# A 28,000-instruction fp32 kernel on one core: the opening, the hand-over to the experts, and the places of the adaptive weights' quarters are rearranged

## What is computed

```python
h = concat([meta, x])                      # 16 + 256 tokens
u = rmsnorm(h, norm_mix_w)
proj = u @ w_in                            # 1024 -> 2064 columns
h = h + concat([pool_mixer(..), gla_mixer(..)]) @ w_out
h = h + hier_moe(rmsnorm(h, norm_ffn_w))   # 4 groups x 4 experts, top 1 group, top 2 experts
x = rmsnorm(h, final_norm_w)[:, 16:]
```

## Time and profile before

| | us |
|---|---|
| median of 3 runs | 2054.75 |
| the runs | 2054.5, 2054.75, 2058.7 |
| the profiled execution | 2057.1 |
| its span, first to last instruction | 2055.3 |
| PE busy in it | 1996.4 |
| DVE busy | 1409.0 |
| ACT busy | 816.3 |

### The profile page before, as it was taken

The page is one execution under the profiler, slowest core; times in us unless marked ns, Lnnn a source line. Parts: engine busy times, 40 slices in busy tenths (PEclk is TensorE's granted clock), DMA queues, the critical chain, the costliest instruction groups (busy, mean ns, idle before and its releaser), DMA issues.

```text
span 2055.3 us, 28217 instructions
## 1 busy us (share of the span) xinstructions
PE 1996.4 (97%) x11259; PEld 1702.3 (83%) x11259; DVE 1409.0 (69%) x1975; ACT 816.3 (40%) x1180; POOL 222.8 (11%) x129
## 2 busy tenths in 40 slices
PE   8989898999999999999999999999999999999998
PEld 7978677888888887579888888988888888689998
DVE  6879996778867569755778867566664346865444
ACT  5354575322222226954222222322222234764443
POOL 0010000000001002531000001000000101333431
PEclk9999999999999999999999999999999999999999
DMA  6557894556645353013656555356564336125654
GB/s 196 162 164 267 297 322 129 172 166 182 172 138 163 114 162 92 16 43 102 175 170 179 161 147 160 97 166 191 172 182 126 99 95 177 46 83 144 185 167 142
DMA packets 415032, 314.40 MB, mean 153 GB/s; under 512 B 27551, under 2 KB 373670, under 8 KB 414902
## 3 DMA queue, kind: packets, MB, share of 16 engines
q1 hardware_dynamic: 375344, 236.97, 39.5%
q10 hardware_dynamic: 39558, 75.64, 11.8%
HBM read 311.51 MB, written 1.05 MB: 152 GB/s over the span
## 4 chain that ended last, share of the span: by engine, by line
PE 85%; DVE 8%; ACT 4%; issue 2%; DMA 1%; ACTq 0%; SPq 0%; DVEq 0%
PE ps L2260 25%; PE ps L2262 24%; PE ps L2261 24%; DVE w_lo L1309 3%; PE ps L2253 2%; PE ps L3069 2%; ACT w_hi L770 2%; PE ps L3036 1%; DVE ada_acc L1335 1%; PE ps L2810 1%; PE ps L2812 1%; PE ps L2841 1%; PE ps L2811 1%; DVE u_lo L1402 1%; DVE tmp_a L1394 1%
## 5 line engine op out<-in xcount | busy, mean ns | idle before, releaser
L2260 PE MATMUL ps<-u_hi,w_hi 128*128 128x512 f32 (+2 forms) x2112 | 738.3, 350 | 13.1 <-DVE u_lo L1402 7.0
L2261 PE MATMUL ps<-u_lo,w_hi 128*128 128x512 f32 (+2 forms) x2112 | 728.5, 345 | 0.0
L2262 PE MATMUL ps<-u_hi,w_lo 128*128 128x512 f32 (+2 forms) x2112 | 728.5, 345 | 0.0
L1309 DVE TENSOR_TENSOR w_lo<-raw,w_hi 128x2048 fp32r<-128x2048 f32 (+1 forms) x215 | 451.5, 2101 | 222.2 <-ACT w_hi L770 222.1
L770 ACT CAST w_hi<-raw 128x2048 fp32r<-128x2048 f32 (+1 forms) x215 | 374.9, 1745 | 420.0 <-PE ps L2262 377.8
L2260 PEld LDWEIGHTS ps<-u_hi,w_hi 128*128 128x128 f32 x2112 | 401.0, 190 | 67.7 <-DVE w_lo L1309 8.5
L2262 PEld LDWEIGHTS ps<-u_hi,w_lo 128*128 128x128 f32 x2112 | 400.6, 190 | 47.9
L2261 PEld LDWEIGHTS ps<-u_lo,w_hi 128*128 128x128 f32 x2112 | 401.1, 190 | 46.0
L1335 DVE SCALAR_TENSOR_TENSOR ada_acc<-ada_w,sc_c,ada_acc 128x512 f32<-128x512 f32 x448 | 317.9, 764 | 6.3 <-DMA ada_w<-in_w_ada 0.7
L890 ACT ACTIVATE tmp_a<-ps 128x512 f32<-128x512 f32 (+1 forms) x88 | 47.9, 545 | 563.2 <-PE ps L2262 421.6
L2260 PE MATMUL ps<-hf_hi,w_hi 128*128 128x512 f32 (+1 forms) x770 | 268.7, 349 | 0.4 <-DVE w_lo L1309 0.2
(11 more groups left out here) (399 smaller groups left out, 2057.3 us busy)
## 6 DMA issues: line engine op xcount, KB each, us to landing
ada_w<-in_w_ada ACTq DMA_DIRECT2D x144, 512.0 KB, 3.8
raw<-in_w_ffn_gate SPq DMA_DIRECT2D x88, 512.0 KB, 3.9
raw<-in_w_ffn_up SPq DMA_DIRECT2D x88, 512.0 KB, 5.3
raw<-in_w_in SPq DMA_DIRECT2D x52, 512.0 KB, 4.8
raw<-in_w_ffn_down SPq DMA_DIRECT2D x64, 384.0 KB, 3.6
raw<-in_w_ffn_down SPq DMA_DIRECT2D x64, 320.0 KB, 4.2
raw<-in_w_expert_down SPq DMA_DIRECT2D x26, 512.0 KB, 5.9
raw<-in_w_expert_gate SPq DMA_DIRECT2D x25, 512.0 KB, 5.4
```

The lines of the kernel that those rows point to most:

```text
L1309: tt(low, full, high.bitcast(F32), ALU.subtract).then_inc(lo_done.sem, 1)
L2260: mm(acc, w1, m_hi, start=(first and i == 0), stop=False)
L2261: mm(acc, w1, m_lo, start=False, stop=False)
L2262: ins = mm(acc, w2, m_hi, start=False, stop=(last and i == n - 1))
```

## The change

It has five parts.

1. **Opening.** The weights of the first norm get a load of their own, first on ACT's queue, and their transpose goes with that of the meta rows. The products with ones are gone: ACT squares the rows as they were loaded and sums them in the same instruction, takes the root, DVE the reciprocal, and PE spreads it over the partitions with three small products. PE starts the first unit's high-by-high products as rows come, then transposes the vectors, then does the other two passes. The first unit's high part is made in two halves.
2. **Beside w_in.** Quarters 0 and 1 move from beside the seventh unit to behind the fifth; quarter 2 is done in halves around the head norm; both halves of quarter 3 come after it. A table load of ACT is moved ahead of a wait. The last chunk's output step is no longer cut in two.
3. **w_out.** The third unit is split in halves, and PE starts on the first.
4. **Experts.** Quarters: visit 0 has 5; visits 1, 2 and 3 had (6,7), (8,9) and (10,11,12) and get (6,7,8), (9,10,11) and (12,13,14); visits 4, 5 and 6 had one each and now visit 4 has 15. The loads follow.
5. **Last visits and hand-over.** Some context rows move behind the expert work. The first unit of the feed-forward network opens before the second tile is scattered, the second unit opens behind it by halves, too. The sums of squares move to DVE, and two small products are left of sixteen.

```diff
+            act.dma_start(mix_rows[:, :], dict(a["vec_src"])["norm_mix"]).then_inc(ld_mix, 16)
-            split_hi(0)
-            for k in range(KD):
-                act.wait_ge(rows_out.sem, rows_out.at(2 + k // 2))
-                nc.scalar.activation((win_a if k < 4 else win_b)[:, k % 4, PAD:PAD + T1], h1[:, k, 0:T1],
-                                     ACT.Square).then_inc(n0["sq"].sem, 1)
+            act.wait_ge(ev["mix_out"], 1)
+            open_rows(0, 2)
+            act.wait_ge(raw_full[0], 32)
+            nc.scalar.copy(w_hi[:, 0, 0:UNIT // 2], raw[:, 0, 0:UNIT // 2]).then_inc(ev["open_high"], 1)
+            open_rows(2, 4)
+            nc.scalar.copy(w_hi[:, 0, UNIT // 2:UNIT], raw[:, 0, UNIT // 2:UNIT]).then_inc(hi_done.sem, 1)
+            open_rows(4, KD)
+            for t, spare in enumerate((tmp_a, tmp_b)):
+                nc.scalar.activation(spare.rearrange("p a t -> p (a t)"), x_rows[:, t, :], ACT.Square, accum_out=tok_inv[:, 0, t:t + 1])
...
+            split_hi(1)
+            act.wait_ge(n0["spread"].sem, n0["spread"].at(1))
+            nc.scalar.copy(rstd[:, 0:T1], ps[:, 5, 0:T1]).then_inc(ev["open_factor"], 1)
...
+                if i == 4:
+                    dve.wait_ge(ev["sc_made"], 1)
+                    ada_quarter(0, 0)
+                    ada_quarter(0, 1)
@@ split_lo, and its like in split_hi
+                if u == OUT_THIRD:
+                    dve.wait_ge(ev["first_high"], 1)
+                    tt(low[:, 0:UNIT // 2], full[:, 0:UNIT // 2], high[:, 0:UNIT // 2].bitcast(F32), ALU.subtract).then_inc(ev["first_low"], 1)
+                    dve.wait_ge(hi_done.sem, u + 1)
+                    tt(low[:, UNIT // 2:UNIT], full[:, UNIT // 2:UNIT], high[:, UNIT // 2:UNIT].bitcast(F32), ALU.subtract
+                       ).then_inc(lo_done.sem, 1)
@@ the quarters' places
-        MOE_QUARTERS = (5, 6, 8, 10, 13, 14, 15, 16)
-        VISIT_LOADS = {1: (7, 8), 2: (9, 10), 3: (11, 12), 4: (13,), 5: (14,), 6: (15,)}
+        MOE_QUARTERS = (5, 6, 9, 12, 15, 16)
+        VISIT_LOADS = {1: (7, 8, 9), 2: (10, 11, 12), 3: (13, 14, 15)}
...
-                return [(q // 4, q % 4) for q in range(q0, q1)], {1: 0, 3: 1, 4: 2, 9: 3}.get(n)
+                return [(q // 4, q % 4) for q in range(q0, q1)], {1: 0, 2: 1, 3: 2, 9: 3}.get(n)
@@ ACT, last visits
-                    if v - 1 in CONTEXT_ROWS and v == VISITS - 1:
-                        high_rows("l0a", 0, 0, *CONTEXT_ROWS[v - 1])
-                if v == VISITS - 1:
-                    nc.scalar.activation(root_one[:, :], one, ACT.Sqrt)
...
-                if v - 1 in CONTEXT_ROWS and v < VISITS - 1:
+                if v - 1 in CONTEXT_ROWS:
                     high_rows("l0a", 0, 0, *CONTEXT_ROWS[v - 1])
             tile_high(TILES - 1)
+            nc.scalar.activation(root_one[:, :], one, ACT.Sqrt)
@@ DVE, hand-over
             for k in range(KD):
                 dve.wait_ge(ev["row_sums"], k + 1)
                 tt(h1[:, k, N_META:T1], row_sum(k), h1[:, k, N_META:T1], ALU.add).then_inc(acc_free.sem, 1)
-            split_lo(M1 + 1)
+                if k >= 2:
+                    square_sum(k - 1)
+            square_sum(KD - 1)
@@ PE, hand-over
+            scatter(2, 0, TILES - 1)
             turn_hidden((STEPS - 1,))
-            scatter(2, 0, TILES - 1)
             begin(down_unit(VISITS - 1), None)
             down_part(STEPS - 1, VISITS - 1, True)
             scatter(3, 0, TILES - 1)
+
+            u, g = layers[0]["f1a"]["u0"], layers[0]["f1a"]["g0"]
+            begin(u, None)
+            pe.wait_ge(ev["m_hid"], STEPS)
+            for k in range(KD):
+                open_ffn(0, 0, k)
             for k in range(4):
                 scatter(k, TILES - 1, TILES)
...
+            begin(u + 1, None)
+            pe.wait_ge(acc_free.sem, acc_free.at(st_moe["g0"] + 6))
+            for k in range(KD):
+                open_ffn(1, 0, k)
+                if k == 4:
+                    final_mean()
+            spread_factor("l0a", 0, 6, 1)
+            for i in range(2):
                 for k in range(KD):
-                    pe.wait_ge(n0["lo"].sem, n0["lo"].at(KD * q + k + 1))
...
+                    ins = open_ffn(i, 1, k)
+                ins.then_inc(unit_done.sem, 1)
```

More of the change, by code:

```diff
@@ L933, in _, with open_rows @@
-            act.wait_ge(n0["ms"].sem, n0["ms"].at(n0["n_ms"]))
-            nc.scalar.activation(rstd[:, 0:T1], ps[:, 5, 0:T1], ACT.Sqrt, bias=eps).then_inc(n0["root"].sem, 1)
-            split_hi(1)
+            def open_rows(k0, k1):
+                for k in range(k0, k1):
+                    act.wait_ge(rows_out.sem, rows_out.at(2 + k // 2))
+                    nc.scalar.activation(u_hi[:, k, 0:T1], h1[:, k, 0:T1], ACT.Identity, scale=mix_w[:, k:k + 1]
+                                         ).then_inc(n0["hi"].sem, 1)
@@ L1553, in _ @@
                                       ).then_inc(rows_out.sem, 1)
+            dve.wait_ge(rows_out.sem, rows_out.at(5))
+            dve.wait_ge(ev["mix_out"], 1)
+            mix1 = norm_of["mix1"]
+            for k in range(KD):
+                dve.wait_ge(mix1["hi"].sem, mix1["hi"].at(k + 1))
+                stt(out=u_lo[:, k, 0:T1], in0=h1[:, k, 0:T1], scalar=mix_w[:, k:k + 1], in1=u_hi[:, k, 0:T1].bitcast(F32),
+                    op0=ALU.mult, op1=ALU.subtract).then_inc(mix1["lo"].sem, 1)
@@ L1559, in _ @@
             ins.then_inc(rows_out.sem, 2)
-            split_lo(0)
-            dve.wait_ge(rows_out.sem, rows_out.at(8))
-            mix1 = norm_of["mix1"]
-            for k in range(KD):
-                w0 = VEC["norm_mix"][0] + k
-                dve.wait_ge(mix1["hi"].sem, mix1["hi"].at(k + 1))
-                stt(out=u_lo[:, k, 0:T1], in0=h1[:, k, 0:T1], scalar=vec[:, w0:w0 + 1], in1=u_hi[:, k, 0:T1].bitcast(F32),
-                    op0=ALU.mult, op1=ALU.subtract).then_inc(mix1["lo"].sem, 1)
@@ L1955, in _ @@
                         ada_quarter(*work[0])
+                    if v == VISITS - 1:
+                        for k in range(*CONTEXT_ROWS[v - 2]):
+                            low_row("l0a", 0, 0, k)
                     split_lo(u + 3)
-                    if v - 1 in CONTEXT_ROWS and v == VISITS - 1:
-                        for k in range(*CONTEXT_ROWS[v - 1]):
-                            low_row("l0a", 0, 0, k)
                 for i in steps_of(v):
@@ L1969, in _ @@
                 if v == VISITS - 1:
+                    for k in range(*CONTEXT_ROWS[v - 1]):
+                        scaled_row("l0a", 0, k)
                     hidden_low((STEPS - 1,))
@@ L2710, in turn_rows @@
                 return ins
-            for i in (2, 3):
+            pe.wait_ge(ev["first_low"], 1)
+            need(pe, acc_free, g + 1)
+            for t in range(2):
+                out1_part(2, t, 0, 4)
+            begin(u + 2, None)
+            for t in range(2):
+                ins = out1_part(2, t, 4, KD)
+            ins.then_inc(unit_done.sem, 1)
+            for i in (3,):
                 begin(u + i, g + i)
@@ L2858, in _, with final_mean, open_ffn @@
             n0, e1 = norm_of["l0a"], norm_of["end1"]
-            def final_mean(k):
-                pe.wait_ge(n0["sq"].sem, n0["sq"].at(k + 1))
+            def final_mean():
+                pe.wait_ge(ev["fin_sum"], KD - 1)
                 for t in range(2):
-                    ins = mm(ps[:, 4 + t, 0:1], square_row(k)[:, P * t:P * t + P], ones_d[:, 0:1], start=(k == 0),
-                             stop=(k == KD - 1))
-                ins.then_inc(ev["fin_means"], 1)
+                    ins = mm(ps[:, 4 + t, 0:1], sq_sum[:, SEQ + P * t:SEQ + P * t + P], ones_d[:, 0:1], start=True, stop=True)
+                ins.then_inc(ev["fin_mean"], 1)
+            def open_ffn(i, q, k):
+                u, (c0, c1, v) = layers[0]["f1a"]["u0"] + i, HALVES["l0a"][q]
+                if i == 0:
+                    pe.wait_ge(n0["lo"].sem, n0["lo"].at(KD * q + k + 1))
+                for t in range(2):
+                    ins = products(ps[:, 2 * i + t, c0:c1], u % 2, [up_cols(t, k)], [(u_hi[:, k, c0:c1], u_lo[:, k, c0:c1])],
+                                   c1 - c0, k == 0, k == KD - 1)
+                return ins
             pe.wait_ge(ev["places"], 1)
```

171 lines of the change are left out of this document (100 added, 71 removed).

## The result

The changed kernel takes 2043.66 us (median of 5 runs, 2043.14 to 2045.2) against 2054.75 for the kernel before beside it: a ratio of 0.9933, with a 95% interval of 0.9919 to 0.9948. The medians differ by 11.1 us. The profiled executions have spans of 2042.0 and 2055.3, 13.3 apart; 13.0 was forecast for them.

The account below looks back on a forecast made before the run. PE, busy 1996.4 of 2055.3 us, was taken as the bound, with gains only in its standing, half clock and needless products. Terms 2.2 + 2.1 + 2.0 + 2.8 + 3.9 = 13.0 gave 2042; range 2035.5 to 2049.

Parts of the forecast that it names:

- Opening: Start of the kernel: ACT's chain becomes the longest and unit 1 starts at 24.3 in place of 26.5, 2.2 us won.
- w_in to w_out: Hand-over between these weights: PE's waits of 1.40 and 1.56 for w_out's second and third units shrink, 2.1 us won.
- the 1.2 for the second unit: w_out's second unit: moving quarters 0 and 1 frees DVE earlier, winning 1.2 of PE's 1.40 wait.
- Together 4.3 us at the router, whose chain carries the shift on: Router: gains of the opening and w_out add to 4.3 us, and its latency-bound chain of small steps passes them on.
- Experts: Expert visits 2 to 7: new tables of quarters remove the 3.82 wait and half clock behind it, 2.0 us won.
- The five waits of 8.9: Expert visits 1 to 5: PE's waits of 0.7, 2.0, 2.8, 1.7 and 1.7, 8.9 against 7.4 before.
- half clock would be absent below 2.8: Expert visits: with none of the new waits over 2.8, visit 6's down product was taken to end 2.0 earlier.
- Last visit: Last expert visit: context rows go behind, and the down product starts at 325.9 in place of 329.09, 2.8 us won.
- Hand-over: Experts to feed-forward network: fill, clock and fewer small sums, less unit 1 in halves and three new waits, 3.9 us won.
- The three-quarter visits: Rival, chance 0.2: in visits 1 to 5 waits grow to 11 or 12, 3 lost in place of 2 won, 2047.
- The waits of the hand-over: Rival, chance 0.13: they only move, so last visit and hand-over give 2 or 3 of 6.7, 2046.
- DVE's debt: Slower rival, chance 0.04: in visits 5 to 15 DVE, over about 4 us behind PE, never catches up, 2059.

Follow-up runs that it names:

- sums_back: Changed kernel with the sixteen small sums of squares back on PE and DVE's seven additions of squares gone: 2047.11 us, ratio 0.9953.
- fill_back: Changed kernel with the first half unit of the feed-forward network behind the scatter in place of in front of it: 2047.58 us, ratio 0.9955.
- warm: Changed kernel with nineteen extra unread PE products in the router, before the norm's small sums and before the wait for the logits: 2041.37 us, ratio 0.9919.
- third_back: Changed kernel with w_out's third unit whole again in place of in halves: 2044.43 us.
- counts_first: Changed kernel with PE's three context products behind the counts and positions in place of in front of them: 2045.14 us, ratio 0.9942.
- fold4: Changed kernel with PE's sum of the third adaptive chunk, and DVE's reading of it, in visit 4 in place of visit 3: 2044.67 us, ratio 0.9940.
- thin: Changed kernel in which DVE adds only 256 of 512 columns of three adaptive quarters, so its result differs: 2039.8 us, ratio 0.9922.
- q_back: Changed kernel with the tables of quarters and loads of the kernel before: 2046.41 us, ratio 0.9945.
- after: First profile of the changed kernel itself, nothing further edited: 2043.66 us, ratio 0.9933 to the kernel before.
- again: The changed kernel run and profiled once more, nothing edited: 2044.58 us.
- both: Changed kernel with the unread router products of warm and the head norm's sixteen one-column sums dealt out between products: 2043.21 us, ratio 0.9931.
- q_only: Kernel before with only the new tables of quarters and loads and their order of adaptive sums: 2057.74 us, ratio 1.0000.

## Why the prediction was right, step by step

The total was right to 0.3 us in the span and to 1.7 in the median. So close a fit is luck in part: by the first load of the experts 2.8 of the forecast gain were missing, and visit 0, for which nothing was forecast, gave 2.6. The points count more than the sum.

**Opening, 2.2 forecast, 1.7 measured.** ACT's times came as forecast (squares of 1.04 with 0.19 for each read-out, the second root done at 19.4, the high part of unit 1 at 21.2), but the squares weren't on the path: DVE's reciprocals were ready at 19.7, and PE, which stands nowhere over 0.2 from 14.68 on, came to the spreads at 20.68. Up to 14.68 PE waits for ACT's `u_hi`; from there the path is PE's own work, with DVE's low part of unit 0 ready at 18.5, just as PE comes to it. Unit 1 began at 24.68 where 24.3 was forecast: the third pass gave way 0.2 later, the spreads took 0.86 in place of 0.7, the low-rank products 3.14 in place of 3.0 (the forecast's own terms, 20.5, 0.7 and 3.0, make 24.2). The rest is that unit 1 of the kernel before began at 26.36, 0.15 earlier than the 26.5 that I had read.

**w_in to w_out, 2.1 forecast, 1.2 measured.** The waits of 1.40 and 1.56 went, as said. The step that failed is the 1.2 for the second unit: the spread of 16 products took 3.31 in place of 1.95 at half clock. In all five profiles of this order in which the clock stayed up there this part gave 1.8 to 1.9, with the opening's gain taken off (2.98 - 1.13 in sums_back, 3.47 - 1.62 in fill_back): more than the 1.2. In the changed kernel 0.3 was left. The 0.9 for the third unit was right at the router (2.87 - 1.94).

**"Together 4.3 us at the router, whose chain carries the shift on": wrong, in the size and in the second half.** It was 2.9 there and 1.5 at the first load. A chain bound by latency does carry a shift on, but PE came earlier to a semaphore that did not come as much earlier. It stood for 1.35 in place of 0.45, and then ran at half clock the three context products that stand in PE's queue ahead of the counts. DVE, SP's loads and the experts stood behind those. warm and third_back show both halves of this.

**Visit 0, nothing forecast, 2.6 measured.** I read the waits of the experts from visit 2 on and passed over the one of 2.37 at 144.57 and the stretch behind it (0.50 at 146 to 148). ACT starts on the second unit, as its load lands, 11.0 behind the first issue in the kernel before and 9.8 in the changed one (140.21 - 129.18, 137.46 - 127.67), and the wait is 1.54 with the clock at 1.00. The first of the two comes again: it is 11.0 and 11.4 in the two profiles of the old code, and 9.5 to 10.7 in the changed kernel, its repeat (10.4) and all its variants but counts_first, where ACT itself comes late. Why the load lands earlier no run shows, so this gain was found and not foreseen, and its cause stays open. With waits of 2.13 and 2.26 the clock stayed up, with 2.37 and 2.70 it fell.

**Experts, 2.0 forecast, 1.7 measured, for a reason that was half right.** DVE's sum was the right thing to count, and fold4 and thin show that it sets the pace. The five waits of 8.9 didn't come as listed: PE had 1.85 for `hid`, 1.63 for `ada_red` and 1.46 for `ht_lo`, 4.9 together. The failing step is the sentence that half clock would be absent below 2.8: it came after 1.85 and 1.63. With it PE's loss is 8.0, close to the 8.9 of the sum. The wait of 3.82 and its half clock went, the largest gain of this part.

**Last visit, 2.8 forecast, 3.1 measured.** The waits of 0.44, 2.46 and 0.77 became 1.01; 0.9 was forecast. That is 2.7 of the 3.1; where the other 0.4 came from is open.

**Hand-over, 3.9 forecast, 4.4 measured.** Term by term: the wait and the half clock that the fill removes, 5.1 forecast, and 4.8 net of 1.05 by fill_back; the small sums 3.0, and 2.9 by sums_back. The sums were sized right. The fill isn't as clear: fill_back waits 3.17 where the kernel before waits 1.76, since that one came to the scatter late (the twelve down products ahead of it took 4.4 at half clock, 2.8 in the changed kernel), so its 4.8 is what the fill is worth in the changed kernel and not the gain over the kernel before. The three new waits were 1.05, 1.64 and 0.81 where 1.6, 1.7 and 1.2 were forecast, 1.0 too much. With the measured sizes the terms (4.8, 2.9, less 0.6, 0.7 and 0.8) make 5.6 where 4.4 was gained; the 1.4 by which fill_back's wait is the longer one would cover the difference.

**The rest: the same length.** 1687.0 behind the third unit in both profiles. It was 1686.4 to 1689.4 in the eleven other runs with the changed hand-over or an edit of it.

**The rivals.** The three-quarter visits do pay by the traces, if less than forecast. The waits of the hand-over did not just move. DVE's debt is there but is paid back by visit 9, since the waits from there on are the same in all kernels (0.8, 0.7, 0.6). The half clock of the routing was in none of the cases; by warm it cost 1.0 to 1.6.

## What to carry to other kernels

Making an engine early at a semaphore that doesn't come earlier has a price: PE stands longer, its clock can fall, and the next products on the path pay. Look at what stands behind each wait that your change lengthens, and whether anything harmless can fill it: 5.8 us of real work in front of the scatter were worth 4.8 us, and 2.3 us of unread products in the router about 1. Where another engine sets the pace, neither the wait nor a short stretch at half clock is worth anything (one of nearly 7 us was, 1.0); add up waits and half clock, and if the sum stays the same when you move things, go to the other engine and take work from it.

## What the runs showed of the hardware

- **Half clock after short lulls.** Behind the router's small sums the granted clock fell in all nine profiles in which PE had waited 1.3 to 1.4 in front of them and 0.8 to 1.0 behind, and in none of the five in which the first wait was 0.45 or was filled. In three of the nine (counts_first, q_back, fill_back) it fell before the second wait began, in fill_back 1.2 before, so there the second wait wasn't needed. I had taken 1.74 (no fall) as a safe size. Waits alone give no threshold: after 1.74 and 1.54 in the visits of the kernel before it stayed at 1.00, and in the changed one it fell after 1.85 and 1.63. The Trainium skill, TensorE: Matmul & The Clock Gate, section "A second HAM failure mode: psum-queue depth-cycling", tells of a kernel in which small pauses between groups of products made the clock swing between its two levels. The rows of the router agree with that: waits of 1.35 and 1.02, and a granted clock of 0.50 over 122 to 124.
- **The same code can fall or not.** Behind 90, where PE does sixteen one-column products (1.92), the clock fell to half in five profiles of ten. Behind the wait for `hid` of 1.8 to 1.9 in visit 1, which ten profiles have with the same code in the experts, it fell in four (after, again, third_back, both) and stayed up in six; behind or within the wait of 2.5 for `ada_red` it fell in four, and not in counts_first and q_only. The routing's stretch, once begun, lasted 3 to 4 us in three profiles and about 10 in six. In fold4 it was still there at 128:

```profile
128.00:130.00 2.00, 2.00 (x6) 1.55 (x6) 1.31 (x7) 1.51 (x3) 0.00 (x0) 0.50 0.48 121
```

- **The start.** Eight products of 272 columns, 13 us after the start, took 2.04 in the kernel before and 3.53 in q_only, with the same code up to there, and everything behind them came 1.4 later.
